# Scoring a decode step's index keys and searching its threshold inside the prompt's attention instead of behind it

## The reference

```python
kidx_past = cache_kidx[page_table].reshape(B, past, IDX_DIM)          # 8 x 4096 x 64
kidx_all = jnp.concatenate([kidx_past, k_idx], axis=1)
dots = jnp.einsum("bqhd,bld->bqhl", q_idx, k_idx) * (IDX_DIM ** -0.5)  # 8 index heads
s = jnp.einsum("bqh,bqhl->bql", w_idx * (N_IDX_HEADS ** -0.5), jax.nn.relu(dots))
_, sel = lax.top_k(scores, n_sel)                                     # n_sel = 256
att = attend_selected(q, k_sel, v_sel, sel <= pos[None, :, None])
mo = mem_attend(z["q_mem"], mem_k, mem_v)                             # 256 memory tokens
```

## Time and profile before

| what | value |
| --- | --- |
| time, median of 3 runs (range) | 2410.22 us (2407.86 to 2412.36) |
| profiled execution, its own time | 2410.6 us |
| its span | 2408.8 us |
| mean granted TensorE clock | 0.900 |
| TensorE busy | 2116.4 us, 88% |
| VectorE busy | 1404.0 us, 58% |
| ScalarE busy | 1200.8 us, 50% |
| GpSimd busy | 113.5 us, 5% |

### The profile page before, as it was taken

One profiled execution on the slowest core, in us unless ns is written; L12 is line 12 of the kernel. 1 busy time (PEld: TensorE's weight loads), 2 busy tenths in 40 slices (PEclk: granted clock), 3 DMA queues, 4 the chain that ended last, 5 costly groups with the idle time before them and its releaser, 6 DMA issues. The chain is left out here.

```text
span 2408.8 us, 33367 instructions
## 1 busy us (share of the span) xinstructions
PE 2116.4 (88%) x12592; PEld 1698.6 (71%) x12592; DVE 1404.0 (58%) x3150; ACT 1200.8 (50%) x2337; POOL 113.5 (5%) x174
## 2 busy tenths in 40 slices
PE   7999999989996889889999878999989989979765
PEld 4776676767765767666778658786777868759662
DVE  2334775676643565657866755697576352625680
ACT  1102467777741346466666765566656675422000
POOL 0000000000000000000000000000000000010004
PEclk9999999999996789989999997999988898977556
DMA  7213121221114212120211010110110001032001
GB/s 277 78 52 104 61 75 63 71 69 61 47 48 154 98 48 66 54 67 12 73 59 57 20 58 33 38 53 8 54 42 20 27 21 45 29 135 85 1 4 33
DMA packets 61888, 144.57 MB, mean 60 GB/s; under 512 B 14288, under 2 KB 28536, under 8 KB 60704
## 3 DMA queue, kind: packets, MB, share of 16 engines
q1 hardware_dynamic: 59552, 131.95, 16.5%
q0 software_dynamic: 2176, 10.49, 1.3%
HBM read 100.18 MB, written 42.24 MB: 59 GB/s over the span
## 5 line engine op out<-in xcount | busy, mean ns | idle before, releaser
L1576 PE MATMUL psum<-sb_v,sb_ptb 128*128 128x64 f32 x2176 | 323.0, 296 | 35.3 <-ACT sb_ptb L1179 34.5
L1576 PEld LDWEIGHTS psum<-sb_v,sb_ptb 128*128 128x128 f32 x2176 | 309.5, 218 | 48.8 <-ACT sb_ptb L1179 48.1
L817 PE MATMUL psum<-sb_w,sb_xt 128*128 128x512 f32 (+5 forms) x1088 | 333.9, 463 | 0.5 <-DVE sb_xt L550 0.5
L1179 ACT ACTIVATE sb_ptb<-psum 128x512 f32<-128x512 f32 (+3 forms) x352 | 183.2, 536 | 225.3 <-PE psum L1568 221.2
L817 PEld LDWEIGHTS psum<-sb_w,sb_xt 128*128 128x128 f32 (+1 forms) x1088 | 180.8, 187 | 125.5 <-issue 113.2
L1568 PE MATMUL psum<-sb_con,sb_p 128*128 128x128 f32 x1280 | 222.6, 298 | 49.7 <-ACT sb_p L1198 36.2
L1351 DVE CUSTOM_DVE_ANT_0 sb_p<-psum,sb_bias 128x1024 f32<-128x1024 f32 (+7 forms) x128 | 126.7, 990 | 203.0 <-PE psum L1558 162.7
L856 PE MATMUL psum<-sb_xt,sb_w 128*128 128x128 f32 x2048 | 237.3, 276 | 0.0
L856 PEld LDWEIGHTS psum<-sb_xt,sb_w 128*128 128x128 f32 x2048 | 234.3, 192 | 1.1
L1600 PE MATMUL psum<-sb_wo,sb_mix 128*128 128x512 f32 x512 | 231.9, 596 | 0.0
L295 ACT ACTIVATE sb_lowj<-sb_sc,sb_l_ncand,sb_l_scl 128x1152 bf16<-128x1152 f32 (+7 forms) x128 | 219.7, 1717 | 4.1 <-DVE sb_l_step L256 2.1
(11 more groups left out here) (408 smaller groups left out, 2953.6 us busy)
## 6 DMA issues: line engine op xcount, KB each, us to landing
qt_s<-sb_qt SPq DMA_DIRECT2D x32, 512.0 KB, 2.9
sb_x<-in_x_prompt SPq DMA_DIRECT2D x16, 512.0 KB, 4.6
xt_s<-sb_xt SPq DMA_DIRECT2D x16, 512.0 KB, 2.6
sb_qa<-qt_s SPq DMA_DIRECT2D x16, 512.0 KB, 4.4
sb_qa<-qt_s SPq DMA_DIRECT2D x32, 256.0 KB, 5.8
sb_xres<-in_x_prompt SPq DMA_DIRECT2D x16, 512.0 KB, 4.4
out_y_prompt<-sb_y SPq DMA_DIRECT2D x16, 512.0 KB, 3.0
sb_p<-xt_s SPq DMA_DIRECT2D x9, 512.0 KB, 5.7
```

Of the source, the lines that this page charges most:

```text
L817: mm = pe.matmul(out, m.xt[:, p, k, 0:n], m.w1[:, k, lo:hi], start=(k == 0), stop=(k == KD - 1))
L1179: act.activation(m.ptb[:, g, 0:cols], m.turn[slot][:, 0:cols], ACT.Copy).then_inc(s.t_act, 1)
L1576: mm = pe.matmul(o, m.ptb[:, g, x * P:(x + 1) * P], v, start=st, stop=sp)
```

## The change

The index keys leave stage C. A unit is 8 blocks of 64 key columns on 128 partitions: four transposes, one copy of 512 columns, four products of 64 columns, and on VectorE a ReLU times weight and a sum over 256 columns. 32 such units go into the heads of steps 0 to 2, at most two in a head, between a head's scores and its own transposes (`KEYS_IN`); VectorE takes a head's units at the start of the next head (`take_keys`). The small products of the sample's queries and weights come behind the first tail (`first_prepare`, `first_products`, `first_copies`). The gathers become 16 pieces of 512 KB through 3 buffers which are cut from memory that early steps don't use; GpSimd issues 9 before step 0 and 7 inside its work for step 0.

The 32 rounds of the search go into heads 0 to 6 of steps 3 to 6 and four heads of step 7: the count on VectorE ahead of the head's own search passes, the sum on TensorE behind the head's transposes, and the bit on VectorE at the start of the next head.

Stage C keeps the rest. On TensorE its order is now: nine small transposes, all z products in one run, the transposes of the memory keys, and then the offset products. Five constants move to loads of their own on SyncE's queue, two of which, with the sample's projections, stand first in stage B. The scaling of the memory output moves from head 1 to head 0, and `normalise` to head 3 in all steps.

```diff
+PAGE_KEYS, PAGE_UNITS, PAGE_PIECES = 16, 2 * PAGE // 8, 2 * PAGE // 16
+KEYS_IN = {0: (0, 1, 2, 2, 2, 2, 2, 2), 1: (0, 1, 2, 2, 2, 2, 2, 2), 2: (0, 1, 2, 2, 1, 0, 0, 0)}
+ROUNDS_IN, ROUNDS = range(3, 8), BITS + 1
...
@@ b_sync
+    sp.dma_start(m.dsx[:], io.ds_s).then_inc(s.c_first, 16)
+    sp.dma_start(m.con[3][:], io.con[3]).then_inc(s.c_first, 16)
     load_qi(EARLY)
     load_xt2(0)
+    sp.dma_start(m.con[4][:], io.con[4]).then_inc(s.c_blk, 16)
...
@@ b_pool
+    def gather_keys(pieces):
+        for n in pieces:
+            g, q = n // (PAGE // PAGE_KEYS), n % (PAGE // PAGE_KEYS)
+            if n >= 3:
+                pool.wait_ge(s.t_done, turns.of[("k", 2 * (n - 3) + 1)][1])
+            pool.indirect_dma_start(out=m.kp3[n % 3], out_offset=None, in_=pages,
...
+    gather_keys(range(9))
     for j in range(NT):
-        if j == NT - 1:
-            pool.wait_ge(s.s_last, NT)
-            gather_pages(pool, m, s, io, range(4))
...
         pool.tensor_tensor(m.yrs[:], m.yms[:], m.rms_con2[:, 2:3], ALU.pow).then_inc(s.yms, 1)
+        if j == 0:
+            gather_keys(range(9, PAGE_PIECES))
         pool.wait_ge(s.y_norm, j + 1)
...
@@ b_vector
+    def take_keys(units):
+        if units:
+            dve.wait_ge(s.pv, groups.of[("k", units[-1])][1])
...
+    def decode_round(j, h):
+        n = round_at(j, h - 1)
+        if n is not None:
+            dve.wait_ge(s.cnt_out, n + 1)
+            if n == 0:
+                search_start(dve, m, cf)
+            else:
+                search_bit(dve, m, cf, n - 1)
...
+        n = round_at(j, h)
+        if n is not None:
+            search_count(dve, m, s, cf, None if n == 0 else m.cc)
...
         for h in range(NH):
+            if h >= 1:
+                take_keys(key_units(j, h - 1))
+            decode_round(j, h)
             behind(j, portion(todo, NH, h), False, h + 1 if h + 1 < NH else None)
-            if h == 1:
+            if h == 0:
...
-            if h == (6 if j < 6 else 3) and j >= 1:
+            if h == 3 and j >= 1:
                 normalise(j - 1)
...
@@ b_tensor
+    def decode_total(j, h):
...
+            pe.wait_ge(s.mo, j + 1)
+            pe.wait_ge(s.cnt_in, n + 1)
+            pe.matmul(m.tot, m.part("blk"), m.cn, start=True, stop=True).then_inc(s.cnt_out, 1)
+
+    def turn_keys(n):
+        if n % 2 == 0:
+            pe.wait_ge(s.k_ld[n // 2 % 3], 16 * (n // 6 + 1))
+        turn_group(("k", n), m.kp3[n // 2 % 3], 512 * (n % 2), 4)
+
+    def times_keys(n):
+        area, g = key_area(n), n // (PAGE // 8)
+        pe.wait_ge(s.mo, key_step(n) + 1)
+        if n - area > 0:
+            pe.wait_ge(s.d_rd, n - area)
+        times_v(("k", n), [(m.kbank[area][:, 64 * x:64 * x + 64], m.qb[:, g, :], True, True) for x in range(4)])
...
     tail(-1)
+    first_products()
...
+        if j == 0:
+            pe.wait_ge(s.c_qb, 1)
...
             if h + ahead < NH:
                 scores_of(j, h + ahead)
+            for n in key_units(j, h):
+                turn_keys(n)
+                if before:
+                    before()
+                before = lambda n=n: times_keys(n)
             pe.wait_ge(s.exp, NH * j + h + 1)
...
+            decode_total(j, h)
...
@@ c_tensor (the key units and the 32 rounds are gone)
+    for n in range(8 * KD):
+        b, k = n // KD, n % KD
+        mm = pe.matmul(m.bank[3][:, 8 * b:8 * b + 8], m.w2[:, k, b * P:(b + 1) * P], m.xts[:, k, :],
+                       start=(k == 0), stop=(k == KD - 1))
+    mm.then_inc(s.c_z, 1)
+    pe.wait_ge(s.c_mk, 16 * DB)
+    for n in range(8):
+        if n >= 2:
+            pe.wait_ge(s.mk_ev, n - 1)
...
     pe.wait_ge(s.c_sel, 1)
     pe.matmul(m.bank[5][:, 4:6], con("blk"), m.cn[:], start=True, stop=True)
```

More of the change, by code:

```diff
@@ L116 @@
     ("newbias", 8),
+    ], [
+    ("sel", 2 * 128),
+    ("diag8", 64),
     ("last", 1),
+    ], [
+    ("blk", 128),
 ]]
@@ L942, with key_units, round_at @@
 DIRECT = NT - 2
+PAGE_KEYS, PAGE_UNITS, PAGE_PIECES = 16, 2 * PAGE // 8, 2 * PAGE // 16
+KEYS_IN = {0: (0, 1, 2, 2, 2, 2, 2, 2), 1: (0, 1, 2, 2, 2, 2, 2, 2), 2: (0, 1, 2, 2, 1, 0, 0, 0)}
+ROUNDS_IN, ROUNDS = range(3, 8), BITS + 1
+NW = PAGE + 1
+def key_units(j, h):
+    if j not in KEYS_IN:
+        return range(0)
+    first = sum(sum(n) for a, n in KEYS_IN.items() if a < j) + sum(KEYS_IN[j][:h])
+    return range(first, first + KEYS_IN[j][h])
+def round_at(j, h):
+    n = (NH - 1) * (j - ROUNDS_IN[0]) + h
+    return n if j in ROUNDS_IN and 0 <= h < NH - 1 and n < ROUNDS else None
 TAIL = 8
@@ L1481, in b_vector @@
     tail(-1)
+    first_copies(dve, m, s, cf)
     dve.wait_ge(s.gp_ld, 16)
@@ L1666, in b_tensor, with key_step, key_area, first_prepare @@
                 mm.then_inc(s.t_done, 1)
-        times_values(j, *before)
+        before()
         tail(j)
-PIECES = 8
-QSLOT = PAGE // 4
 GROUPS = 2 * PAGE // 4
-NW = PAGE + 1
+def key_step(n):
+    return max(j for j in KEYS_IN if key_units(j, 0).start <= n)
+def key_area(n):
+    j = key_step(n)
+    return next(n - units.start for units in (key_units(j, h) for h in range(NH)) if n in units)
+def first_prepare(dve, m, s, ch):
+    dve.wait_ge(s.c_first, 32)
+    con, x = m.part, m.dsx
+    qidx = x[:, 512:1024].rearrange("b (h d) -> b h d", h=NIH)
+    ch.inc(dve.tensor_copy(m.qd[:], qidx.unsqueeze(2).to_broadcast([DB, NIH, 2, HD])))
+    ch.link(dve.tensor_tensor(m.prod[:], qidx, x[:, 1280:1344].unsqueeze(1).to_broadcast([DB, NIH, HD]), ALU.mult))
+    wb = x[:, 1344:1352].unsqueeze(1).to_broadcast([DB, DB, NIH])
+    ch.inc(dve.tensor_tensor(m.wd[:].rearrange("b (r h) -> b r h", r=DB),
+                             con("diag8")[0:DB].rearrange("b (r h) -> b r h", r=DB), wb, ALU.mult))
+    ch.link(dve.tensor_reduce(m.nd[:], m.prod[:], AX, ALU.add))
+    ch.link(dve.scalar_tensor_tensor(out=m.nd[:], in0=m.nd[:], scalar=0.0, in1=x[:, 1344:1352], op0=ALU.max,
+                                     op1=ALU.mult))
+    ch.link(dve.tensor_reduce(m.snew[:], m.nd[:], AX, ALU.add))
+    dve.sem_inc(s.c_row, 1)
+    for g in range(2):
+        ch.inc(dve.memset(m.qb[:, g, :], 0.0))
+    ch.wait()
@@ new lines, in first_copies @@
+def first_copies(dve, m, s, ch):
+    dve.wait_ge(s.c_small, 1)
+    small, last = m.kbank[0], m.part("last")
+    for par in range(2):
+        rows = slice(64 * par, 64 * par + 64)
+        src = small[rows, 0:64].rearrange("p (h b) -> p b h", h=NIH)
+        for g in range(2):
+            ch.inc(dve.tensor_copy(m.qb[rows, g, 32 * par:32 * par + 32].rearrange("p (b h) -> p b h", b=4),
+                                   src[:, 4 * g:4 * g + 4, :]))
+    ch.inc(dve.tensor_copy(m.wrow[:], small[:, 64:128].rearrange("p (g n) -> p g n", g=2)))
+    ch.inc(dve.tensor_scalar(m.nlast[:], last, 1.0, -NEG, ALU.subtract, ALU.mult))
+    ch.link(dve.tensor_scalar(m.scd[:, :, PAGE], small[:, 128:130], last, None, ALU.mult))
+    ch.link(dve.tensor_scalar(m.scd[:, :, PAGE], m.scd[:, :, PAGE], m.nlast[:], None, ALU.add))
+    dve.sem_inc(s.c_qb, 1)
```

302 lines of the change are left out of this document (113 added, 189 removed).

## The result

The changed kernel takes 2458.82 us (median of 4 runs, 2455.62 to 2465.43); before 2409.04. The ratio is 1.0211, with an interval of 1.0182 to 1.0240: slower by 50 us, where I forecast 26 us faster, and above the range. On another chip the same kernel later gave 1.0133 (1.0052 to 1.0214); three of its four runs took 2461 us and one 2429. The profiled execution has a span of 2454.6 us against 2408.8.

A forecast was written before the change was run, and what follows sets the result against it. TensorE was taken as fullest in the prompt, and a TensorE-VectorE ping-pong as the bound of stage C's search. 2410.6 - 88.9 (stage C) + 39.2 (keys) + 23.1 (rounds) = 2384.0 us, range 2354 to 2418.

The forecast's parts named there:

- Stage C: After the barrier, without key units and rounds: 88.9 us saved, z taking 27.5 us, offsets waiting for TensorE's queue.
- The rival of a released z stream: Stage C: unbroken z leaves the low clock, 14.8 us for 27.5; chance 0.21 together with better heads.
- Keys in steps 0 to 2: Heads of steps 0 to 2: 41.0 + 5.9 - 12.0 us for 32 key units, plus 4.3 for the first chain.
- the first chain: Before step 0's memory values: 12 small products and VectorE's copies, put at 4.3 us.
- the rival of the cold units: Steps 0 to 2: the other 27 units also stay at the low clock, 31.9 us more, total 2420; chance 0.13.
- five cold units: Heads of steps 0 to 2: the first five key units at the low clock, 5 x 1.18 = 5.9 us.
- the price of the rounds: Heads of steps 3 to 7: 32 search rounds lengthen them by 23.1 us.
- half of the 0.74 as met: Steps 3 to 7: half of VectorE's 0.74 us wait for each total is paid, 11.8 us over 32 rounds.
- the lower bound: Steps 3 to 7: 11.3 us, where VectorE's busy time plus the rounds exceeds the heads' length.
- the upper bound: Steps 3 to 7: every round bare, 32 x 2.08 = 66.6 us.
- steps 8 to 15: Prompt steps behind the rounds: nothing moved from step 8 on, 0 us.
- The rival with the bare rounds: Steps 3 to 7: each head's mask waits for the whole round, 66.6 us for 23.1, total 2427.5; chance 0.08.

The follow-up runs named there:

- e12: The changed kernel run again, unchanged, on another chip; 1.0133 of the kernel before (1.0052 to 1.0214).
- e15: Changed kernel without the rounds' totals and VectorE's waits for them, and normalise at head 7 in steps 3 to 7; 0.9986 of the kernel before.
- e3: Changed kernel with each round behind the next head's search pass and mask on VectorE, TensorE's total one head later; 1.0106 of the kernel before.

## Why the prediction was wrong

- Stage C: right. 87.8 saved against 88.9, z at 1.2 GHz in 27.3 us against 27.5, the offsets bound by TensorE's queue. The rival of a released z stream did not come. The Trainium skill (TensorE: Matmul & The Clock Gate, Part 1: The HAM clock gate) has activity release the throttle; here an unbroken stream of products of 8 columns stayed at 0.50, and the measurement decides.
- Keys in steps 0 to 2: the size was right in the first profile alone (36.9 against 34.9, and 6.9 against 4.3 for the first chain once stage A's 5.4 are taken off), and that was luck: in the fifteen profiles of the experiments the same stretch is 44 to 55 us longer than before. The windows over it, after and in e12 (columns as in the earlier trace rows):

```profile
811.52:1032.13 220.61, 201.48 (x1268) 166.96 (x1268) 141.75 (x333) 112.23 (x248) 20.83 (x23) 0.93 0.26 77
```

```profile
809.44:1044.05 234.61, 217.53 (x1268) 183.02 (x1268) 142.97 (x333) 112.15 (x248) 20.78 (x23) 0.86 0.25 72
```

  TensorE does the same instructions in 16 us more at a lower clock; in e12 the heads of step 0, with 13 units, stand at 0.50 throughout. So the rival of the cold units came in part, and five cold units were too few. No wait of TensorE for a gather shows in either.
- The step that failed is the price of the rounds: "half of the 0.74 as met, 32 x 0.37 = 11.8, on top of the lower bound: +23.1". It measured 68, above even the upper bound of 66.6: 45 of the 72 us by which the forecast missed the spans (steps 8 to 15, put at nothing, are another 16). I let VectorE's work count only where its sum was longer than the head, and took the heads with their ends (31 us of window on average for 24 from the first to the last maximum), in which VectorE's idle time is longer. Between these maxima VectorE has 33 us free for 43 of work, and not all of it usable: in e15, 31 of the 43 us lengthen the steps, against the 11.3 of the lower bound. The totals cost 17 to 26 against 11.8, and VectorE's waits for them are not half of 0.74 us in each head but 13 long ones (us in all, times, longest):

```profile
DVE sb_few L1873 <- PE psum L1679: 25.4, 13, 5.1
```

  The collisions were in no bound; taking them away, and the normalisation beside them, brought 11 to 20 us.
- The rival with the bare rounds had the right side and nearly the right price for them (66.6 for 68); I gave it 0.08. Its price was luck: by its mechanism each mask waits for a whole round, and with the round behind the mask (e3) 49 us stayed. The collisions I charged at nothing, since I looked only at how much work there was. It is not the move of the normalisation to head 3 alone that brought them: in steps 6 and 7 it stood at head 3 before too, and the long instruction is there as well.
- Steps 8 to 15 took 16 us more with the same instructions, 15 in e12, and 3 to 12 in the other runs that leave these steps unchanged. The windows over the whole stretch, before and after, show TensorE busy for 17 us more with as many instructions at a clock lower by 0.02:

```profile
1352.86:2113.18 760.32, 678.84 (x4275) 574.60 (x4274) 451.61 (x801) 470.46 (x771) 27.54 (x33) 0.91 0.11 35
```

```profile
1470.09:2246.76 776.67, 696.28 (x4275) 590.79 (x4275) 451.33 (x800) 470.34 (x771) 26.43 (x32) 0.89 0.11 34
```

So it is TensorE's clock; why it was lower stays open. So does why the order of the round made no difference in steps 3 to 7.

## What to carry to other kernels

Before a small serial job goes into a busy loop, add up the free time of its engine within the loop alone, without the ends, and price the job as bare where that is short (33 us for 43 here, 68 us lost); where there was nearly three times the room the same rounds cost 6 to 24. Take a second profile before you call a stretch right: the first one here had the shortest steps 0 to 2 of sixteen. Before you call a moved instruction free, look at what runs on its neighbours at its new place, GpSimd beside VectorE above all. When work leaves a gap that hid other work, reorder what is left: the stream that was hidden becomes the wait.

## What the runs showed of the hardware

An instruction of VectorE on 256 numbers took 2.36 us in place of 0.23 beside GpSimd's addition; taking five such meetings away, and the normalisation in front of them, gave 20 us with the totals and 11 without, for 10.6 us of their own. An unbroken run of 128 TensorE passes of 8 columns stayed at a granted clock of 0.50 for 27.3 us. The same work in the heads of step 4 took 25.99 us at a granted clock of 0.80 in one run and 32.71 at 0.55 in another.
